# An encoder block on one core: wider passes reordered, expert 0's token ranks computed first, first transposes in two banks

## The reference, cut to what matters

```python
def reference(x, ...):                       # x: (1, 1024, 1024)
    u = rms_norm(h, norm1_g); proj = u @ w_in
    conv_out = conformer_conv_group(...)     # GLU, causal depthwise conv (31), LayerNorm, silu
    attn_out = swa_sink_attention(...)       # 8 heads of 64, window of 128 frames
    h = h + concat(conv_out, attn_out) @ w_out
    v = rms_norm(h, norm2_g)
    return h + moe(v, ...)

def moe(xf, router_w, router_b, w1, b1, w2, b2):      # 32 experts, top 4, d_ff 1024
    top_val, top_idx = top_k(xf @ router_w + router_b, 4)
    gates = softmax(top_val)
    # each token's 4 experts, weighted by the gates:
    #   h = xb @ w1 + b1;  x_glu = min(h[:, :1024], 7);  x_lin = clip(h[:, 1024:], -7, 7)
    #   y = (x_glu * sigmoid(1.702 * x_glu) * (x_lin + 1)) @ w2 + b2
```

## Time and profile before

| | us |
|---|---|
| median of 3 runs | 2062.84 (2062.68 to 2063.18) |
| profiled execution | 2062.79 |
| its span | 2061.1 |
| TensorE busy | 1963.7 |
| VectorE busy | 991.2 |
| ScalarE busy | 450.6 |
| GpSimd busy | 227.8 |

### The profile page before, as it was taken

How to read it: one execution, slowest core, us unless ns; L and a number is a source line. 1 busy time by engine, 2 the same in 40 slices (tenths; PEclk the granted TensorE clock), 3 DMA queues, 4 the chain that set the end, 5 groups by cost and what they waited for, 6 DMA issues and landing times.

```text
span 2061.1 us, 35334 instructions
## 1 busy us (share of the span) xinstructions
PE 1963.7 (95%) x13245; PEld 1623.0 (79%) x13246; DVE 991.2 (48%) x2416; ACT 450.6 (22%) x982; POOL 227.8 (11%) x222
## 2 busy tenths in 40 slices
PE   6999989959999999999999999999999999979997
PEld 3555545437888878888778888999999999979996
DVE  3998862354454545544544544444444433323332
ACT  3166564111111111111111111211111111111111
POOL 3111100010101001101001010101111110110001
PEclk9999989969999999999999999999999999989998
DMA  6000115336989999989999999888888888785651
GB/s 234 1 1 1 58 45 208 116 144 246 343 312 347 335 346 343 336 320 345 336 343 346 312 344 330 298 306 286 294 296 294 289 271 270 269 282 200 214 179 42
DMA packets 233941, 509.11 MB, mean 247 GB/s; under 512 B 7997, under 2 KB 12633, under 8 KB 233888
## 3 DMA queue, kind: packets, MB, share of 16 engines
q1 hardware_dynamic: 215264, 447.97, 60.5%
q0 software_dynamic: 16768, 59.98, 10.6%
q10 hardware_dynamic: 1856, 0.41, 0.1%
HBM read 475.53 MB, written 32.80 MB: 247 GB/s over the span
## 4 chain that ended last, share of the span: by engine, by line
PE 91%; DVE 4%; issue 2%; ACT 1%; DMA 1%; POOL 1%; SPq 0%; ACTq 0%; DVEq 0%; POOLq 0%
PE bank L1109 48%; PE bank L1149 12%; PE bank L1124 10%; PE bank L1342 6%; PE bank L1220 5%; PE bank L1482 2%; DVE arena L855 2%; PE bank L1256 2%; PE bank L1267 1%; PE bank L1137 1%; PE bank L1473 1%; PE bank L1138 1%; PE bank L1293 1%; DMA arena<-in_x 0%; PE bank L1212 0%
## 5 line engine op out<-in xcount | busy, mean ns | idle before, releaser
L1109 PE MATMUL bank<-arena 128*128 128x128 f32 (+5 forms) x8192 | 996.9, 284 | 24.5 <-issue 24.5
L1109 PEld LDWEIGHTS bank<-arena 128*128 128x128 f32 x8192 | 987.8, 192 | 37.1 <-issue 37.1
L754 DVE TENSOR_SCALAR arena<-bank,b1c 128x256 f32<-128x256 f32 x256 | 123.7, 483 | 477.6 <-PE bank L1109 477.0
L464 ACT ACTIVATE arena<-arena 128x256 f32<-128x256 f32 x256 | 106.6, 417 | 868.5 <-DVE arena L754 868.5
L1149 PE MATMUL bank<-arena 128*128 128x512 f32 x576 | 262.1, 593 | 0.0
L1124 PE MATMUL bank<-arena 128*128 128x144 f32 (+4 forms) x1792 | 252.0, 294 | 4.6 <-DVE arena L766 4.4
L1081 DVE TENSOR_SCALAR arena<-bank,cols 128x256 f32<-128x256 f32 x256 | 112.0, 479 | 283.5 <-PE bank L1482 283.5
L1124 PEld LDWEIGHTS bank<-arena 128*128 128x128 f32 x1792 | 237.1, 190 | 7.7 <-DVE arena L766 7.7
L352 POOL DMA_INDIRECT out<-arena,idx_cur x64 | 99.0, 1547 | 873.4 <-DVE arena L798 863.6
L855 DVE SCALAR_TENSOR_TENSOR arena<-arena,cols 128x512 f32<-128x512 f32 (+1 forms) x226 | 182.2, 806 | 16.3 <-ACT arena L557 9.4
L1149 PEld LDWEIGHTS bank<-arena 128*128 128x128 f32 x576 | 102.4, 190 | 94.7 <-issue 90.4
(11 more groups left out here) (220 smaller groups left out, 1104.8 us busy)
## 6 DMA issues: line engine op xcount, KB each, us to landing
arena<-in_w SPq DMA_DIRECT2D x192, 2048.0 KB, 11.4
arena<-in_b SPq DMA_DIRECT2D x32, 512.0 KB, 11.0
arena<-in_x SPq DMA_DIRECT2D x16, 512.0 KB, 6.8
token_rows<-arena SPq DMA_DIRECT2D x8, 528.0 KB, 2.9
out<-arena SPq DMA_DIRECT2D x8, 512.0 KB, 6.0
arena<-in_w_in SPq DMA_DIRECT2D x2, 1536.0 KB, 13.4
arena<-in_w_in SPq DMA_DIRECT2D x1, 3072.0 KB, 19.8
arena<-in_w_out SPq DMA_DIRECT2D x1, 2048.0 KB, 8.4
```

What stands on the lines that cost most here:

```text
L464: a.activation(sg[:, m % 2, :], g1[:, m % 2, :], ACT.Sigmoid, scale=ALPHA).then_inc(sg_ready, 1)
L754: v.tensor_scalar(g1[:, r, :], bank[r][:, 0:SLOTS], b1c[:, m:m + 1], LIMIT, ALU.add, ALU.min).then_inc(g1_ready, 1)
L1109: last = mm(bank[m % 2][:, side * SLOTS:side * SLOTS + n], w1_sb[:, k, lo:lo + P], xT[:, k, 0:n], start=k == 0, stop=k == KD - 1)
```

## The change

The diff below is cut; beside it, the gather gets one semaphore for each half in place of one for both, and every waiter waits for both halves, except the first transposes.

- Router: at t = 8 `fold_logits(6)` comes before the wait for tile 7's normalized rows, no longer behind its transposes.
- Rank products: each waits for its own mask; those of tiles 0 to 6 come first, and those that need the last mask are nine at the end.
- Ranks: VectorE computes those of expert 0 alone, then one-hots; the copy `pos` comes behind them and the ranks of all experts behind the table.
- First transposes: banks 6 and 7 in turn, the first half of the slots as soon as it is there; the table product comes after two of the four rounds, and the last round behind the load of the lap count.
- Hidden layer: the wait for all of `xT` becomes four waits, for two k-tiles each, in the first block's first side.
- VectorE: `hidden_b(6)` before `hidden_a(7)`, in every pass.
- Wider passes: `down(7)` directly behind `down(6)`, then `trans_y` 4 to 7, then `trans_x(3)`.

```diff
@@ dve_pass
             for m in range(1, MT):
                 hidden_a(m)
-                hidden_b(m - 1)
+                if m < MT - 1:
+                    hidden_b(m - 1)
+                if m == MT - 2:
+                    hidden_b(m)
@@ the scalar engine, first xT
-                    last = a.activation(xT[:, k, :], bank[6][:, (k % 2) * SLOTS:(k % 2 + 1) * SLOTS], ACT.Copy,
+                    last = a.activation(xT[:, k, :], bank[6 + i % 2][:, (k % 2) * SLOTS:(k % 2 + 1) * SLOTS], ACT.Copy,
@@ the vector engine
             v.wait_ge(rank_mm, 1)
-            v.tensor_copy(pos[:].rearrange("p t e -> p (t e)"), bank[0][:, 0:NT * NE])
+            pos_mm = bank[0][:, 0:NT * NE].rearrange("p (t e) -> p t e", e=NE)
             link(v.tensor_copy(nE[:], bank[0][:, NT * NE:NT * NE + NE]))
-            link(v.tensor_tensor(rka[:], tokid[:].unsqueeze(2).to_broadcast([P, NT, NE]), pos[:], ALU.subtract))
-            link(v.tensor_tensor(rka[:], rka[:], nE[:].unsqueeze(1).to_broadcast([P, NT, NE]), ALU.add))
-            link(v.tensor_tensor(rkd[:], pos[:], rka[:], ALU.subtract))
-            link(v.tensor_tensor(rkd[:], rkd[:], Mf[:], ALU.mult))
-            link(v.tensor_tensor(rank[:], rka[:], rkd[:], ALU.add))
+            link(v.scalar_tensor_tensor(rka[:, :, 0], tokid[:], nE[:, 0:1], pos_mm[:, :, 0], ALU.add, ALU.subtract))
+            link(v.tensor_tensor(rkd[:, :, 0], pos_mm[:, :, 0], rka[:, :, 0], ALU.subtract))
+            link(v.tensor_tensor(rkd[:, :, 0], rkd[:, :, 0], Mf[:, :, 0], ALU.mult))
+            link(v.tensor_tensor(r8[:], rka[:, :, 0], rkd[:, :, 0], ALU.add))
...
-            link(prep(rank[:, :, 0], 0.0))
             one_hots()
+            v.tensor_copy(pos[:], pos_mm)
@@ pe_pass
-            pe.wait_ge(xt_ev, q4)
             for m in range(MT):
...
                     for k in range(KD):
+                        if m == 0 and side == 0 and k % 2 == 0:
+                            pe.wait_ge(xt_ev, q4 - 3 + k // 2)
...
             down(6, range(MT))
-            trans_y(4)
+            down(7, range(MT))
+            for d in range(4, KD):
+                trans_y(d)
             trans_x(q4, 3)
-            down(7, range(MT))
-            trans_y(5)
-            trans_y(6)
-            trans_y(7)
@@ the tensor engine
+                if t == NT:
+                    fold_logits(NT - 2)
                 if 1 <= t <= NT:
...
-                if t >= 2:
+                if 2 <= t < NT:
                     fold_logits(t - 2)
...
-            pe.wait_ge(mask_ready, NT)
+            def rank_terms(t, us):
+                for u in us:
+                    pe.wait_ge(mask_ready, u + 1)
+                    last = mm(bank[0][:, t * NE:(t + 1) * NE], tri_b[:] if u == t else ones_b[:], Mb[:, u, :],
+                              start=u == 0, stop=u == min(t, NT - 1))
+                return last
+
             pe.wait_ge(h_ready, NT)
-            for t in range(NT + 1):
...
+            for t in range(NT - 1):
+                rank_terms(t, range(t + 1))
+            rank_terms(NT, range(NT))
+            rank_terms(NT - 1, range(NT)).then_inc(rank_mm, 1)
...
-            pe.wait_ge(gath_in, 32)
-            for i in range(4):
-                trans_x(0, i)
+
+            def first_x(i, h):
+                if i >= 2 and h == 0:
+                    pe.wait_ge(xt_ev, i - 1)
+                for k in (2 * i, 2 * i + 1):
+                    last = pe.transpose(bank[6 + i % 2][:, (k % 2) * SLOTS + h * P:(k % 2) * SLOTS + (h + 1) * P],
+                                        gath[:, h, k * P:(k + 1) * P], ident[:])
+                if h == 1:
+                    last.then_inc(xt_mm, 1)
+
+            for h in range(2):
+                pe.wait_ge(gath_in[h], 16)
+                for i in range(2):
+                    first_x(i, h)
             pe.wait_ge(diag_ready, 2)
             mm(bank[1][:, 0:5 * TQ + 4], ones_f[:], diag[:], start=True, stop=True).then_inc(tab_mm, 1)
-
-
+            for h in range(2):
+                first_x(2, h)
             pe.wait_ge(tab_ready, 1)
             n_laps = pe.value_load(tabI[0:1, 4 * TQ + 1:4 * TQ + 2], min_val=1, max_val=2)
+            for h in range(2):
+                first_x(3, h)
```

More of the change, by code:

```diff
@@ L220, in hybrid_block @@
         w2_in = [sem(f"w2_in{c}") for c in range(2)]
-        oh_ready, idx_mm, idx_ready, gath_in = sem("oh_ready"), sem("idx_mm"), sem("idx_ready"), sem("gath_in")
+        oh_ready, idx_mm, idx_ready = sem("oh_ready"), sem("idx_mm"), sem("idx_ready")
+        gath_in = [sem(f"gath_in{h}") for h in range(2)]
         xt_mm, xt_ev, cur_ready = sem("xt_mm"), sem("xt_ev"), sem("cur_ready")
@@ L313, in _ @@
             sp.wait_ge(wo_mm, 2 * NT)
-            sp.wait_ge(gath_in, 32)
+            for h in range(2):
+                sp.wait_ge(gath_in[h], 16)
             for c in range(2):
@@ L778, in dve_pass @@
                         v.wait_ge(added[i], q * 16 + 16)
-                    v.wait_ge(gath_in, q * 32 + 32)
+                    for h in range(2):
+                        v.wait_ge(gath_in[h], q * 16 + 16)
                     v.tensor_copy(idx_cur[:], idx_next[:])
@@ L1086, in _ @@
             v.sem_inc(sg_free, 2)
+            link(v.tensor_tensor(rka[:], tokid[:].unsqueeze(2).to_broadcast([P, NT, NE]), pos[:], ALU.subtract))
+            link(v.tensor_tensor(rka[:], rka[:], nE[:].unsqueeze(1).to_broadcast([P, NT, NE]), ALU.add))
+            link(v.tensor_tensor(rkd[:], pos[:], rka[:], ALU.subtract))
+            link(v.tensor_tensor(rkd[:], rkd[:], Mf[:], ALU.mult))
+            link(v.tensor_tensor(rank[:], rka[:], rkd[:], ALU.add))
             for i in range(4):
@@ L1155, in pe_pass @@
                 down_rows(0, range(4))
-                pe.wait_ge(gath_in, q32 + 32)
+                for h in range(2):
+                    pe.wait_ge(gath_in[h], q16 + 16)
                 pe.wait_ge(idx_ready, q + 2)
@@ L1458, in _ @@
             fold_logits(NT - 1)
-            pe.wait_ge(mask_ready, NT)
-            pe.wait_ge(h_ready, NT)
-            for t in range(NT + 1):
-                for u in range(min(t, NT - 1) + 1):
-                    own_tile = u == t
-                    last = mm(bank[0][:, t * NE:(t + 1) * NE], tri_b[:] if own_tile else ones_b[:], Mb[:, u, :],
-                              start=u == 0, stop=u == min(t, NT - 1))
-            last.then_inc(rank_mm, 1)
+            def rank_terms(t, us):
[4 more added lines that the diff above has]
+                return last
+            pe.wait_ge(h_ready, NT)
+            for t in range(NT - 1):
+                rank_terms(t, range(t + 1))
+            rank_terms(NT, range(NT))
+            rank_terms(NT - 1, range(NT)).then_inc(rank_mm, 1)
             def slots_to_tokens(n):
```

2 lines of the change are left out of this document (1 added, 1 removed).

## The result

The changed kernel takes 2036.31 us (2036.02 to 2036.66, 4 runs) against 2063.01 of the kernel before beside it: a ratio of 0.987, interval 0.9853 to 0.9887. That is 26.7 us off. The span went from 2061.1 to 2034.3.

The account below looks back on a forecast made before the run. TensorE was taken as the bound, nine tenths of the span, leaving only idle time to win. Start 7.4, activation 4.4, boundaries 7.0, less 0.9 in the last pass: 17.9 us off 2062.8, so 2044.9, range 2038.5 to 2052.

Parts of the forecast that it names:

- seventh activation: Wide passes, before the down projection: doing this activation during the eighth block removes TensorE's idle wait, 4.4 us in all.
- the jump: Change from 152 to 176 columns, over the 160-wide code: the 13.13 us stall stays if the number of code blocks stays.
- Start: Ahead of the first pass: five terms together bring the first hidden matmul 7.4 us earlier, from 6.4 to 8.
- Term (d): Ahead of the first pass: table product placed between the first transposes, starting right behind its columns, gains 3.4 us.
- Term (e): Between table and first pass: 3.22 us of count loading stay; the last transposes there cost 0.3 us, bounds 0 to 1.1.
- Clock of the first pass: First hidden half, run at half clock: its extra 3.0 us stay as they are, plus or minus 0.6.
- The pass's end: Boundaries behind wide passes: last transposes behind the down projection save 0.54 us each, 7.0 over 13, bounds 2.6 to 8.5.
- Rival 1: Jump over the 160-wide code: one code block fewer on the path gives 2039 to 2040.5 us; chance 0.11.
- Rival 2: Wide-pass boundaries: idle is loop overhead no queue covers, so only the 0.2 us wait goes each time, 2049.3; chance 0.09.
- Rival 3: Start gains 2 us less: gather waits for the row store, or transposes stand in full, 2047; chance 0.05.
- Rival 4: Adjacent width changes: resident code falls out of reach, 11.4 us more each; two give 2067.8, three 2079; chance 0.03.
- Rival 5: Passes: hidden_a(7) late by the early activation and the last xT not there in time, about 2054 us; chance 0.04.

Follow-up runs that it names:

- b_start: The kernel before with only the part ahead of the first pass changed, passes as before: 2056.34 us, ratio 0.9964.
- a_tablelast: The changed kernel with the table product behind all four rounds of first transposes again: 2035.83 us, ratio 0.9865.
- b_end: The kernel before with only the wide passes' end reordered and the wait for xT in four parts: 2052.21 us, ratio 0.9943.
- the two paddings: Never-run transposes added to the 160-wide code: ten on the kernel before, 2060.18 us; 119 on the changed kernel, 2039.26 us.
- b_end_fullwait: The kernel before with the wide passes' end reordered, but one wait for all of xT at the pass's head: 2064.88 us, ratio 1.0008.
- a_w2late: The changed kernel with a pass's w2 loads issued behind its first hidden block, not at the end of the pass before: 2033.08 us, ratio 0.9854.
- a_no160: The changed kernel without width 160 in its list, so no code is jumped over: 2026.58 us, ratio 0.9826.

## Why the prediction was wrong, point by point

The direction was right, and so were the mechanisms of the start and of both parts of the wide pass. The sum fell 8.8 us short, and the range's lower end 2.2. Two steps failed: the seventh activation was priced by the idle column, and the jump was left at nothing. By term, the miss is 3.0 at the twelve boundaries, 3.95 at the jump's (4.49 for 0.54), 0.75 and 0.78 of clock, 0.5 at the end, and -0.2. No one of them alone takes the time out of the range: without the 3.0, or without the 3.1 of the missing silent stretch, it would have been about 2039.4.

- **Start, 7.4.** Measured 7.43, and `b_start` gave 7.2 alone. That it fits to the decimal is luck, since where the first pass begins varies by up to 2 us between kernels with the same start; the means of the five old starts (467.06) and the eight new ones (459.63) differ by 7.4 too. Term (d) has the right size under the wrong name: `a_tablelast` shows that the table product's place earns nothing. Term (e) was charged 0.3; from the product to the pass it is 5.43 for 5.24.
- **Clock of the first pass, nothing plus or minus 0.6.** Measured 0.75. In every kernel with the new start of these runs (eight) the first half took 16.2 to 16.8, in the five with the old one 17.4 to 17.7. The trace has the clock at 0.50 from 431.8 to 472.7 before and from 433.0 to 463.7 after, a shorter stretch, so 3.0 to 6.0 us into the pass it is 0.80 on the average, and 0.54 before. The cause stays open. Work of TensorE right before the pass isn't needed for it: `a_tablelast` is idle for 3.94 us there, like the kernel before (3.95), where the changed kernel is for 1.27, and its first half takes 16.40 all the same.
- **Seventh activation, 4.4. This step failed.** Measured 8.3 alone. The mechanism is as told, and nothing waits in its place. What failed is the price of a stall: the idle column of the earlier trace rows was taken for it. Start to start a stall costs some 0.3 us more, 13 times. The prediction had measured the boundary start to start and this one not.
- **The pass's end, 0.54 for each boundary.** Measured 0.56 in `b_end`. Together with the activation they make 13.9 us for twelve boundaries; the forecast had 4.4 + 12 x 0.54 = 10.9.
- **The last pass, a loss of 0.9.** Measured 0.4: from the last down projection's start to the scatter it is 28.62 before and 29.02 after. The four additions take 2.73 in one block where 2.8 was counted, and TensorE's part ends 0.4 earlier than before, of which the activation gives 0.2.
- **The jump, nothing but its boundary's share. This step failed too.** 4.49 us came there. 3.1 of it is the silent stretch, as the two paddings show; 0.3 is a shorter branch (6.22 for 6.55), and 1.1 is what the neighbouring boundaries gain as well. The loads of the counts took the same in sum (1.72 for 1.76). Rival 1, one block of code fewer on the path (chance given: 0.11), is what happened. Its price, 4.4, came from dividing 13.13 by three blocks of which only two lie in the stall, so that the total came out near is luck; the block measured 2.8 to 3.6. What was dismissed was that "a few waits among many hundred instructions" could decide; 18 did. The range took rival 1 in alone, not together with the errors of the other terms.
- **The clock behind the jump, nothing.** Measured 0.78. It doesn't come from the block, since neither padding moved it by more than 0.12. `b_end` has it too (21.03 for 21.87). Why stays open.
- **Rival 2, the boundary as mere loop overhead:** refuted by `b_end`. **Rival 3, a later gather:** refuted, the rows were in at 450.2 as forecast. **Rival 4, adjacent code falling out of reach:** refuted, TensorE's idle time at those changes is 1.4 to 1.5 us, below the 1.69 before. **Rival 5:** not so here, but `b_end_fullwait` shows that it is exactly what the order without the partial waits does.

## What to carry to other kernels

Price a stall of TensorE by the distance between the starts on either side less the usual pitch, not by the idle column. Where a loop's code is chosen by branches, look for long branches and silent stretches of the sequencer before you move anything: a jump over code that isn't resident cost TensorE 9 to 13 us here, its size changed by 3 us with 18 instructions that have nothing to do with it, and leaving out one unused width removed it. Compare TensorE's own idle time, not the chain's: a chain that arrives through another engine shows the same stall shorter. And a wait that is split by what each part needs is what makes a moved step free.

## What the runs showed of the hardware that I had not expected

- The listed duration of a 128-column float32 record is 0.27 to 0.29 us at a pitch of 0.11 to 0.12, so idle before a record is listed some 0.15 us too small, and the second record behind a stall comes 0.1 us late (0.227 behind the stall at 1547.63).
- A branch on TensorE over the 160-wide code: 6.0 to 6.8 us in ten kernels with weights in flight, 3.4 in the one without (`a_w2late`), 0.09 where the code is adjacent (`a_no160`). A missing second block: 2.8 to 3.6 us more, in five kernels.
- A count loaded into a register takes 0.30 us with nothing else in flight (`a_w2late`) and up to 1.47 with transfers in flight (`b_end`).
- An idle stretch of 1.7 us at the change to 152 columns let the granted clock fall (0.57 over four us in `b_start`) in two of the four profiles that have it, and cost 1.7 us each time.
